# Four small expert rounds in plain fp32 with two column halves side by side, in the order L S L L S L S S

## The chip, the core and the metric

The kernel runs on one core of a Trainium2 chip. TensorE (PE), VectorE (DVE), ScalarE (ACT), GpSimd (POOL) and SyncE (SP) each run their own instruction stream and meet through semaphores; sixteen DMA engines move data between HBM and the core's memory. The metric is the device time of one execution, in microseconds, lower is better; the figure is the median of several runs.

## The reference

Two layers of a decoder trunk on 256 tokens of width 1024, all in float32. Layer 0 is attention (a dilated and a grouped-query part) and a dense SwiGLU of width 3584. Layer 1 is a gated linear recurrence and a mixture of eight SwiGLU experts, of which the router takes two for each token. What the change touches is the last part:

```python
def moe_swiglu(h, w_router, w_gate, w_up, w_down):
    ...
    logits = (t @ w_router).astype(jnp.float32)
    top_v, top_e = lax.top_k(logits, TOP_K)          # TOP_K = 2
    gates = jax.nn.softmax(top_v, axis=-1)
    ...
    def expert_block(args):                          # xb: rows of tokens, e: their expert
        xb, e = args
        return (jax.nn.silu(xb @ w_gate[e]) * (xb @ w_up[e])) @ w_down[e]
    ...
    y = yb.reshape(P, D)[dest] * g_sorted[:, None].astype(t.dtype)
    out = jax.ops.segment_sum(y, tok_sorted, num_segments=N)
```

An expert has three matrices of 1024 x 3584 floats, 44 MB together, and all eight are read: 352 MB. The result must agree with a float32 reference, so the kernel cannot round a factor to fewer bits and leave it there.

## The kernel before, in words

*The weight stream.* Every matrix is cut into units of 1 MB (128 partitions x 2048 floats). SyncE loads unit after unit into a ring of seven raw buffers (`raw`, `RAW = 7`, `load` at line 394; the transfer is line 408). A raw buffer may be overwritten when VectorE has split the unit that lay in it (`lo_done`).

*The split.* TensorE takes a float32 factor exactly in three fast passes if each factor is split into a high part, rounded to the fast format (`F32R`), and the rest. ScalarE copies each half of a unit to `w_hi` (lines 802 and 807), VectorE subtracts to get `w_lo` (lines 1229 and 1234). The split units lie in a ring of three (`SPL = 3`). `split_to(k)` on both engines makes them split ahead of TensorE by up to three units; PE's semaphore `unit_done` gives back a place.

*The products.* `triple` (lines 1870 to 1872) makes one product as high x high, high x low and low x high: three instructions with a stationary tile of 128 token rows and 512 streamed weight columns. A unit is four such products, 12 instructions. `pair` (lines 1876, 1877) does two instructions: where a block has at most 64 tokens, the high and the low part of the rows lie side by side in the 128 stationary columns, so that high and low of the weights are streamed once each, 8 instructions a unit, and the two halves of the output are added later.

*Rounds.* The router's counts put the experts in descending order of their tokens (`perm`; a place is a rank in this order). A round is one expert: 28 units of gate and up, then 14 units of down. Large rounds have 128 slots for tokens, small ones 64 (`HALF`). Before the change the places from 5 on are small (`SMALL_FROM = 5`), with up and down packed and gate as a triple. `phase` runs the gate and up products of the next round and the down products of the one before, interleaved from the fourth pair on: two gate or up units, one down unit. The order of rounds is written out in `BEFORE_LOOP`, `LOOP_PLACE` and `BEHIND_LOOP`: L S L, then the loop, which runs once when all counts fit their slots and nine times when one doesn't, then S L S L. Between the rounds GpSimd fetches the next round's token rows from HBM by an indirect DMA (`fetch`, line 669), PE transposes them (`row_transposes`), ScalarE copies the finished results to `ybuf` (`results`), and GpSimd stores them to `done` (`store_large`, line 679; `store_small`, two stores of which the second adds to the first, lines 690 and 692). At the end the other rounds' results are fetched back (line 739), weighted and added to X by VectorE (line 1812). The last round isn't stored: its results are brought to the token rows by a product with a one-hot matrix `ST`, in two fast parts (lines 2469 and 2473), and added (line 1825). Then follow the final norm and four stores of the output (line 471).

*Hidden rows.* The product silu(gate) x up of a round lies in `H` as rows; PE transposes it four blocks at a time (`expert_transposes`, line 2083), ScalarE and VectorE make `h_hi` and `h_lo` of it.

Plain float32 products exist before the change too: the weighting with `V` in attention (lines 2020 and 2022: 64 stationary columns, outputs in partitions 0-63 and 64-127 of one bank) and the sums with `ones` in the recurrence (line 2266). The profile records each plain float32 product as two instructions.

Of the kernel before, what the change touches and what calls it, by code (L numbers as in the profile page):

```python
# [75 lines left out]
FIRST_BLOCK = (0, 4, 5, 2, 15, 1, 3, 14)  # L76
# [4 lines left out]
SMALL_COL = BLOCKS  # L81
LAST_COL = 2 * BLOCKS
# [9 lines left out]
def behind_pair(pair):  # L92

    return 2 * (pair + 1) + max(0, pair - LAG)

# [9 lines left out]
class Tally:  # L105
# [3 lines left out]
    def __init__(self):  # L109
        self.count, self.per, self.var, self.rounds = {}, {}, None, 0  # L110
# [10 lines left out]
    def enter(self, var, per):  # L121
        self.var, self.per, self.start = var, per, dict(self.count)

    def leave(self, rounds):
# [3 lines left out]
        self.count, self.var = dict(self.start), rounds  # L128
# [16 lines left out]
def build(nc, x, positions, g_mix, g_ffn, g_final, w_in_attn, w_out_attn, attn_sinks, w_in_rec,  # L145
# [3 lines left out]
    with ctx:  # L149
# [36 lines left out]
        ST = sb("ST", [P, TOK], F32R)  # L186
# [17 lines left out]
        half_row = sb("half_row", [P, 2, 14], I32)  # L204
# [8 lines left out]
        behind_wait = sb("behind_wait", [P, 1], U32)  # L213
        token_now = sb("token_now", [P, 1], U32)
# [39 lines left out]
        y_hi = [t_lo[:, 4 * m:4 * m + 4, 0:CAP] for m in range(2)]  # L254
        y_lo = [t_lo[:, 4 * m:4 * m + 4, CAP:2 * CAP] for m in range(2)]
        beside = w_at(7680, 512).rearrange("p (s c n) -> p s c n", s=2, n=HALF)
        summed = w_at(8192, 512).rearrange("p (s c n) -> p s c n", s=2, n=HALF)
        h_pack = h_hi[:].rearrange("p s (c two n) -> p s c two n", two=2, n=HALF)
# [14 lines left out]
        back = [[w_at(5632, D), w_at(6656, D)], [w_at(10240, D), w_at(11264, D)]]  # L273
# [61 lines left out]
        y_half, yh_done, part_sq, bias_set = sem("y_half"), sem("yh_done"), sem("part_sq"), sem("bias_set")  # L335
# [5 lines left out]
        beside_done, sum_done, half_stored = sem("beside_done"), sem("sum_done"), sem("half_stored")  # L341
# [20 lines left out]
        for first in (2 * D, 3 * D):  # L362
            for nb in range(2):
# [3 lines left out]
        U0 = len(stream)  # L367
        assert FFN_UNITS % RAW == 0 and FFN_UNITS % SPL == 0
# [5 lines left out]
                     unit=FFN_UNITS)  # L374
# [12 lines left out]
        def _(sp):  # L387
            n = Tally()
# [4 lines left out]
            def load(src, k):  # L393

                seen = n.step("unit")
                if k >= RAW:
                    sp.wait_ge(lo_done, n.at("unit", RAW))
# [29 lines left out]
            def load_pair(e, pair, at):  # L427

                for h in range(2):
                    load(expert_unit(2 * pair + h, e), at + h)  # L430

            def load_phase(e_down, e_next):

                at = U0 + GU
                for pair in range(2 * FB):
                    load_pair(e_next, pair, at)
                    at += 2
                    if pair >= LAG:
                        load(expert_unit(GU + pair - LAG, e_down), at)
                        at += 1  # L440
                for j in range(2 * FB - LAG, DOWN):
                    load(expert_unit(GU + j, e_down), at)
                    at += 1

# [3 lines left out]
            e_down = 0  # L448
            for place, _ in BEFORE_LOOP[1:]:
                e_next = sp.value_load(perm[0:1, place:place + 1], min_val=0, max_val=NE - 1)  # L450
                load_phase(e_down, e_next)
                e_down = e_next
            before = sp.value_load(nrounds[0:1, 0:1], min_val=1, max_val=NE + 1)
            with sp.Fori(0, before) as i:
                n.enter(i, {"unit": FFN_UNITS})
                load_phase(sp.value_load(turn_of[0:1, bass.ds(i, 1)], min_val=0, max_val=NE - 1),
                           sp.value_load(turn_of[0:1, bass.ds(i + 1, 1)], min_val=0, max_val=NE - 1))
                n.leave(before)
            e_down = sp.value_load(turn_of[0:1, bass.ds(before, 1)], min_val=0, max_val=NE - 1)
            for place, _ in BEHIND_LOOP:  # L460
                e_next = sp.value_load(perm[0:1, place:place + 1], min_val=0, max_val=NE - 1)
                load_phase(e_down, e_next)
                e_down = e_next
            for j in range(DOWN):
                load(expert_unit(GU + j, e_down), U0 + GU + j)
# [10 lines left out]
        def _(pool):  # L476
# [36 lines left out]
            for m in range(2):  # L513
# [1985 lines left out]
```

## Time and profile before

| | |
|---|---|
| median of 3 runs | 1420.44 us (1420.31 to 1422.4) |
| the profiled execution, first to last instruction | 1416.6 us |
| mean granted TensorE clock in it | 0.997 |
| PE busy | 1384.1 us, 98% |
| VectorE busy | 1201.1 us, 85% |
| ScalarE busy | 997.2 us, 70% |
| DMA traffic | 452.48 MB, mean 319 GB/s |
| expert rounds, from the first gate product | about 513 to 1406 us |

A busy share is the union of an engine's instructions. PE's matmuls overlap in their pipeline, so the duration of one is longer than the distance to the next; what a matmul costs in a stream is the distance of starts. The page cuts the span in 40 slices of 35.4 us; the windows view gives busy time, clock, DMA share and GB/s for any stretch. A wait names the engine, the instruction that waited, and who released it.

### The profile page before, as it was taken

To read this page: it belongs to the slowest core of one execution; us is meant where nothing else is said; L and a number is where in the kernel's file an instruction comes from. 1 tells how busy PE (TensorE), PEld (TensorE's weight loads), DVE (VectorE), ACT (ScalarE), POOL (GpSimd) and SP (SyncE) were. 2 spreads that over 40 slices of the span, in tenths; PEclk is the share of its full clock that TensorE was granted. 3 is DMA by queue.
4 is the path that set the end of the run, shared out by engine and by line. 5 is a ranking of instruction groups with operands and counts; after the bars stand their busy time and mean duration, and the time that the engine had idled before them with its cause. 6 is when DMAs were issued, how large, how long until landed. Compare 5 with 4: busy or idle time off the path is not lost.

```text
span 1416.6 us, 19280 instructions
## 1 busy us (share of the span) xinstructions
PE 1384.1 (98%) x6746; PEld 1146.6 (81%) x6746; DVE 1201.1 (85%) x1455; ACT 997.2 (70%) x1247; POOL 165.1 (12%) x206
## 2 busy tenths in 40 slices
PE   8989999999999999999999999999999999999997
PEld 6858888888988887888888788888888878887876
DVE  7876554544887679999999999999999999999898
ACT  7666444444632577788888877788888888888885
POOL 1000200000244048300010000010020010010002
PEclk9999999999999999999999999999999999999999
DMA  9526785554543459999999999999999999999994
GB/s 333 203 66 203 289 335 183 201 175 154 179 149 110 158 142 393 403 409 409 410 408 410 409 407 406 387 375 410 406 412 412 407 406 413 409 411 414 399 415 155
DMA packets 134174, 452.48 MB, mean 319 GB/s; under 512 B 9514, under 2 KB 18818, under 8 KB 119744
## 3 DMA queue, kind: packets, MB, share of 16 engines
q1 hardware_dynamic: 126752, 433.09, 79.6%
q0 software_dynamic: 5456, 17.06, 3.3%
q10 hardware_dynamic: 1872, 1.12, 0.3%
q8 instruction: 54, 0.88, 0.2%
q14 instruction: 40, 0.33, 0.1%
HBM read 438.90 MB, written 14.17 MB: 320 GB/s over the span
## 4 chain that ended last, share of the span: by engine, by line
PE 76%; DVE 10%; DMA 3%; issue 3%; ACT 2%; DVEq 0%; ACTq 0%; SPq 0%
PE bank L1870 22%; PE bank L1872 21%; PE bank L1871 21%; DVE w_lo L1234 4%; DVE w_lo L1229 4%; DMA raw<-in_w_gate_moe_dram 3%; PE bank L1876 3%; PE bank L1877 3%; PE bank L2083 2%; PE bank L2258 1%; ACT w_hi L802 1%; DVE work L1493 1%; ACT w_hi L807 1%; PE bank L1891 1%; PE bank L2073 0%
## 5 line engine op out<-in xcount | busy, mean ns | idle before, releaser
L802 ACT ACTIVATE w_hi<-raw 128x1024 fp32r<-128x1024 f32 x411 | 435.4, 1059 | 352.5 <-PE bank L1872 325.7
L1229 DVE TENSOR_TENSOR w_lo<-raw,w_hi 128x1024 fp32r<-128x1024 f32 x411 | 506.1, 1231 | 145.0 <-ACT w_hi L802 143.7
L1234 DVE TENSOR_TENSOR w_lo<-raw,w_hi 128x1024 fp32r<-128x1024 f32 x411 | 506.7, 1233 | 0.1
L1870 PE MATMUL bank<-w_hi,t_hi 128*128 128x512 f32 (+1 forms) x1088 | 430.8, 396 | 2.4 <-DVE w_lo L1234 1.6
L807 ACT ACTIVATE w_hi<-raw 128x1024 fp32r<-128x1024 f32 x411 | 429.8, 1046 | 0.2 <-DMA raw<-in_w_in_attn_dram 0.2
L1871 PE MATMUL bank<-w_lo,t_hi 128*128 128x512 f32 (+1 forms) x1088 | 421.9, 388 | 0.0
L1872 PE MATMUL bank<-w_hi,t_hi 128*128 128x512 f32 x672 | 262.5, 391 | 0.0
L1870 PEld LDWEIGHTS bank<-w_hi,t_hi 128*128 128x128 f32 x1088 | 205.2, 189 | 44.7 <-issue 2.8
L1871 PEld LDWEIGHTS bank<-w_lo,t_hi 128*128 128x128 f32 x1088 | 204.9, 188 | 40.8 <-issue 1.0
L1872 PE MATMUL bank<-w_hi,t_lo 128*128 128x512 f32 (+1 forms) x472 | 182.3, 386 | 0.0
L1870 PE MATMUL bank<-w_hi,h_hi 128*128 128x512 f32 x408 | 162.7, 399 | 2.0 <-DVE w_lo L1229 1.6
L1872 PE MATMUL bank<-w_hi,h_lo 128*128 128x512 f32 x408 | 159.5, 391 | 0.0
L1871 PE MATMUL bank<-w_lo,h_hi 128*128 128x512 f32 x408 | 158.9, 390 | 0.0
L1872 PEld LDWEIGHTS bank<-w_hi,t_hi 128*128 128x128 f32 x672 | 126.2, 188 | 27.3
L1872 PEld LDWEIGHTS bank<-w_hi,t_lo 128*128 128x128 f32 x472 | 88.7, 188 | 18.3
L1870 PEld LDWEIGHTS bank<-w_hi,h_hi 128*128 128x128 f32 x408 | 76.7, 188 | 20.4 <-DVE w_lo L1229 3.7
L1872 PEld LDWEIGHTS bank<-w_hi,h_lo 128*128 128x128 f32 x408 | 76.6, 188 | 16.4
L1871 PEld LDWEIGHTS bank<-w_lo,h_hi 128*128 128x128 f32 x408 | 76.7, 188 | 14.8
L1876 PE MATMUL bank<-w_hi,h_hi 128*128 128x512 f32 x168 | 66.8, 398 | 4.8 <-ACT ST L1109 2.8
L1877 PE MATMUL bank<-w_lo,h_hi 128*128 128x512 f32 x168 | 65.9, 392 | 0.0
L676 POOL TENSOR_TENSOR slot_now<-slot_at,unit_of 128x1 uint32<-128x1 uint32 x4 | 5.0, 1260 | 412.5 <-ACT work L1093 412.5
L1876 PE MATMUL bank<-w_hi,t_hi 128*128 128x512 f32 x112 | 43.7, 390 | 0.0
(368 smaller groups left out, 1373.1 us busy)
## 6 DMA issues: line engine op xcount, KB each, us to landing
raw<-in_w_gate_moe_dram SPq DMA_DIRECT2D x112, 1024.0 KB, 9.3
raw<-in_w_up_moe_dram SPq DMA_DIRECT2D x112, 1024.0 KB, 9.5
raw<-in_w_down_moe_dram SPq DMA_DIRECT2D x112, 1024.0 KB, 9.7
raw<-in_w_in_rec_dram SPq DMA_DIRECT2D x16, 1024.0 KB, 5.5
raw<-in_w_gate_dense_dram SPq DMA_DIRECT2D x14, 1024.0 KB, 5.2
raw<-in_w_up_dense_dram SPq DMA_DIRECT2D x14, 1024.0 KB, 5.1
raw<-in_w_down_dense_dram SPq DMA_DIRECT2D x14, 1024.0 KB, 4.9
raw<-in_w_in_attn_dram SPq DMA_DIRECT2D x8, 1024.0 KB, 14.9
```

What stands on the lines that cost most here:

```text
L802: act.activation(w_hi[:, (u - 1) % SPL, half], raw[:, r, half], ACT.Copy).then_inc(hi_half, 1)
L807: act.activation(w_hi[:, (u - 1) % SPL, half], raw[:, r, half], ACT.Copy).then_inc(hi_done, 1)
L1229: dve.tensor_tensor(w_lo[:, s, half], raw[:, r, half], w_hi[:, s, half].bitcast(F32), ALU.subtract).then_inc(lo_half, 1)
L1234: dve.tensor_tensor(w_lo[:, s, half], raw[:, r, half], w_hi[:, s, half].bitcast(F32), ALU.subtract).then_inc(lo_done, 1)
L1493: dve.tensor_tensor(hb, hb, bank[up_bank][:], ALU.mult).then_inc(free[up_bank], 1)
L1870: pe.matmul(o, lh, rh, start=start, stop=False)
L1871: pe.matmul(o, lh, rl, start=False, stop=False)
L1872: return pe.matmul(o, ll, rh, start=False, stop=stop)
L1876: pe.matmul(o, packed, rh, start=start, stop=False)
L1877: return pe.matmul(o, packed, rl, start=False, stop=stop)
L1891: last = pe.transpose(bank[TB[j]][:, c * TOK + t * P:c * TOK + (t + 1) * P], rows_of[:, t, k * P:(k + 1) * P], ident[:])
L2083: last = pe.transpose(bank[b][:, c * P:(c + 1) * P], rows_h[:, c // 2, c % 2, :], ident[:])
```

## The change

The places from 4 on are small, four of eight; the order becomes L S L, the loop, S L S S. A small round no longer splits weights: PE multiplies straight from the raw buffers in plain float32, with 64 token columns as the stationary tile. Each token tile is used for two blocks of weight columns, whose products go to partitions 0-63 and 64-127 of one bank, one instruction behind the other. A list worked out when the program is built (`split_units`) says for each unit whether it is split or direct; ScalarE and VectorE skip the direct ones, SyncE waits for PE's count (`unit_done`) in place of VectorE's before it overwrites them. Rows, hidden rows and results of small rounds are kept in float32 (`t32`, `HS`, `h32`), without a high and a low part and without a sum of two halves. In a small round the results are 64 rows in two halves of the columns, and go out in two plain stores. The three units behind the loop that the loop's body has split ahead stay split, though nobody reads the parts. The last round is small, and its results are brought to the token rows in plain float32 from the two partition halves. Some small tables for the adding stores go.

```diff
-SMALL_FROM = 5
-BEFORE_LOOP = ((0, False), (5, True), (1, False))
+SMALL_FROM = 4
+BEFORE_LOOP = ((0, False), (4, True), (1, False))
 LOOP_PLACE = 2
-BEHIND_LOOP = ((6, True), (3, False), (7, True), (4, False))
-LAST_PLACE = 4
+BEHIND_LOOP = ((5, True), (3, False), (6, True), (7, True))
+LAST_PLACE = 7
...
+            def slot_given_back(k, loop):
...
+                if DIRECT[u]:
+                    sp.wait_ge(unit_done, past + (u + 1))
+                else:
+                    sp.wait_ge(lo_done, past + SPLITS[u])
...
+            def store_small(block):
+
+                for m in range(2):
+                    pool.dma_start(done_h[:, 2 * block, m * BLK:(m + 1) * BLK],
+                                   ybuf[m * HALF:(m + 1) * HALF, 0:BLK]).then_inc(y_stored, 16)
...
+                    if not n.in_loop and not SPLIT[u - 1]:
+                        continue
...
+            def gather_small():
+
+                wait_full(GATE + 1)
+                act.activation(t32, bank[GATE + 1][:], ACT.Copy).then_inc(free[GATE + 1], 1)
...
+            drained(GATE + 1, UP + 1)
+            dve.tensor_tensor(t32.rearrange("p (k n) -> p k n", k=KC), t_hi[:, :, 0:HALF].bitcast(F32),
+                              t_hi[:, :, CAP:CAP + HALF].bitcast(F32), ALU.add).then_inc(t32_done, 1)
...
+            dve.wait_ge(unit_done, n.past(here(DOWN)))
+            dve.tensor_copy(y32[:, BLK // 2:], bank[YLAST[1]][:, 0:BLK // 2]).then_inc(y_right, 1)
...
+            def raw_unit():
+
+
+                r = next_unit()
+                if SPLIT[n.count["at"] - 1]:
+                    pe.wait_ge(lo_done, n.at("split"))
+                pe.wait_ge(loaded[r], n.at(f"loaded{r}"))
+                return r
...
+            def small_down_unit(j):
+
+                if j % 4 == 0:
+                    drained(TR + j // 4 % 2)
+                r = raw_unit()
+                for k in range(2):
+                    for m in range(2):
+                        ws = slice(k * D + m * BLK, k * D + (m + 1) * BLK)
+                        last = pe.matmul(bank[YB][m * HALF:(m + 1) * HALF, :], small_columns(j, k), raw[:, r, ws],
+                                         start=j == 0 and k == 0, stop=j == DOWN - 1 and k == 1)
+                last.then_inc(unit_done, 1)
...
+            def small_pair(at):
...
+                for h in (2 * part, 2 * part + 1):
+                    r = raw_unit()
+                    for i in range(per):
+                        k = h * per + i
+                        for m in range(2):
+                            ws = slice((2 * i + m) * ncols, (2 * i + m + 1) * ncols)
+                            last = pe.matmul(bank[b][m * HALF:(m + 1) * HALF, 0:ncols], t32[:, k * HALF:(k + 1) * HALF],
+                                             raw[:, r, ws], start=k == 0, stop=k == KC - 1)
+                    last.then_inc(unit_done, 1)
...
+            for part, (ready, ns) in enumerate(((y_left, slice(0, BLK // 2)), (y_right, slice(BLK // 2, BLK)))):
+                pe.wait_ge(ready, 1)
                 for t in range(TT):
...
+                    for m in range(2):
+                        ms = slice(m * HALF, (m + 1) * HALF)
+                        last = pe.matmul(bank[LAST[t][m]][:, ns], ST[ms, t * P:(t + 1) * P], y32[ms, ns], start=True,
+                                         stop=True)
```

## Rows read from the trace of the kernel before

**Rows 1.** The page's second part, whole span: GB/s moved, 40 slices of 35.4 us.
```profile
GB/s 333 203 66 203 289 335 183 201 175 154 179 149 110 158 142 393 403 409 409 410 408 410 409 407 406 387 375 410 406 412 412 407 406 413 409 411 414 399 415 155
```
**Rows 2.** Windows, busy time of each engine by round (columns in the first line).
```profile
core 0: us, PE busy (x) PEld busy (x) DVE busy (x) ACT busy (x) POOL busy (x), PEclk, DMA share, GB/s
594.00:704.00 110.00, 109.37 (x500) 90.27 (x499) 107.27 (x103) 92.86 (x104) 0.00 (x0) 1.00 1.02 410
...
812.00:931.00 119.00, 119.00 (x543) 98.94 (x542) 109.71 (x103) 92.78 (x103) 3.93 (x5) 1.00 1.01 396
...
1146.00:1254.00 108.00, 107.40 (x486) 87.95 (x485) 106.50 (x102) 91.61 (x102) 6.26 (x5) 1.00 1.02 409
1254.00:1367.00 113.00, 108.21 (x484) 89.03 (x483) 106.08 (x107) 92.87 (x112) 4.20 (x4) 0.98 1.02 410
...
579.00:1390.00 811.00, 802.54 (x3636) 662.01 (x3635) 780.50 (x758) 673.98 (x770) 48.51 (x41) 1.00 1.02 406
```
**Rows 3.** ScalarE's timeline; a window; loads' time to landing, 1170-1300 us and dense part.
```profile
1200.41 1.06 ACT L802 ACTIVATE w_hi<-raw 128x1024 fp32r<-128x1024 f32 x1 [0.56 <-DMA raw<-in_w_gate_moe_dram]
...
1202.93 1.06 ACT L802 ACTIVATE w_hi<-raw 128x1024 fp32r<-128x1024 f32 x1 [0.51 <-DMA raw<-in_w_gate_moe_dram]
...
1170.00:1215.00 45.00, 45.00 (x205) 37.38 (x204) 44.12 (x42) 38.67 (x43) 0.00 (x0) 1.00 1.02 413
...
raw<-in_w_gate_moe_dram SPq DMA_DIRECT2D x18, 1024.0 KB, 13.6
...
raw<-in_w_up_dense_dram SPq DMA_DIRECT2D x14, 1024.0 KB, 5.1
```
**Rows 4.** Timeline of PE in the all-large round: start us, us, instruction.
```profile
847.50 0.39 PE L1870 MATMUL bank<-w_hi,t_hi 128*128 128x512 f32 x1
...
849.31 0.39 PE L1872 MATMUL bank<-w_hi,t_hi 128*128 128x512 f32 x1
```
**Rows 5.** The end: last load's issue and time to landing, then the engines' timelines.
```profile
1379.94 0.33 SPq L408 DMA_DIRECT2D raw<-in_w_down_moe_dram  x1
...
raw<-in_w_down_moe_dram SPq DMA_DIRECT2D x1, 1024.0 KB, 10.1
...
1405.19 0.39 PE L1872 MATMUL bank<-w_hi,h_lo 128*128 128x512 f32 x1
...
1400.83 5.24 DVE L1812 SCALAR_TENSOR_TENSOR X<-work,row_f,X 128x1024 f32<-128x1024 f32 x4
...
1407.39 2.73 DVE L1825 SCALAR_TENSOR_TENSOR X<-bank,gl,X 128x512 f32<-128x512 f32 x4
...
1412.13 1.81 SPq L471 DMA_DIRECT2D out_dram<-work  x4
```
**Rows 6.** The chain that ended last, at the two products of line 2266.
```profile
406.28 1.72 PE bank L2266 x4
```
**Rows 7.** Timelines of PE and its weight loads in attention; then line 2022's loads.
```profile
103.20 0.65 PE L2020 MATMUL bank<-work 128*64 128x256 f32 x4
103.68 0.39 PE L2022 MATMUL bank<-work 128*64 128x128 f32 x4
104.00 0.50 PE L1870 MATMUL bank<-w_hi,t_hi 128*128 128x512 f32 x1
...
103.47 0.36 PEld L2022 LDWEIGHTS bank<-work 128*64 128x64 f32 x4
...
L2022 PEld LDWEIGHTS bank<-work x32: 137/137/137, 62.6 to 103.7; 128*64 128x64 f32 x32
```
**Rows 8.** Line 739, the fetches of stored results: durations, first and last start, landing.
```profile
L739 POOL DMA_INDIRECT work<-done,row_from x4: 945/1424/1745, 1384.9 to 1390.2; - x4
...
DMA to landing us min/median/max: 5.8/6.0/6.4
```
**Rows 9.** A wait of PE in 1254 to 1367 us, and the window behind it.
```profile
PE bank L1876 <- ACT ST L1109: 2.8, 1, 2.8
...
1308.40:1311.80 3.40, 3.40 (x12) 2.74 (x11) 2.04 (x3) 2.00 (x2) 0.00 (x0) 0.53 1.03 418
```

More of the change, by code:

```diff
@@ L253, in build @@
         ybuf = w_at(4608, D)
[L254 to L258, printed above, removed]
+        t32 = w_at(12416, KC * HALF)
+        h32 = w_at(7680, 2 * BLK).rearrange("p (s n) -> p s n", s=2)
+        HS = w_at(5632, FF // 2)
+        y32 = t32
         key = w_at(10240, NE)
@@ L701, in _, with rows_taken @@
+            def rows_taken(r):
+                return U0 + GU + FFN_UNITS * (r - 2) + 2 * FB * 2 + 2 * FB - LAG
+            large = [sum(1 for small in SMALL_ROUND[:r] if not small) for r in range(LOOP_ROUND + 1)]
+            fetch(FIRST_BLOCK[BEFORE_LOOP[1][0]], 1)
             pool.wait_ge(unit_done, U0 + GU - 1)
             fetch(FIRST_BLOCK[BEFORE_LOOP[2][0]], 2)
-            results_ready(0)
-            store_large(FIRST_BLOCK[BEFORE_LOOP[0][0]], 1)
-            pool.wait_ge(unit_done, rounds_past)
@@ L767, in unit_at @@
             def unit_at(k):
[L768 to L769 removed]
+                return n.past(k + n.rounds * FFN_UNITS)
             def saw_product(*banks):
@@ L1093, in results @@
+            def gather_small():
+                wait_full(GATE + 1)
+                act.activation(t32, bank[GATE + 1][:], ACT.Copy).then_inc(free[GATE + 1], 1)
+            def results(small, stored_before):
+                act.wait_ge(y_stored, n.step("stored", stored_before))
+                banks = 1 if small else 2
+                saw_product(*(YB + m for m in range(banks)))
+                act.wait_ge(unit_done, n.past(here(FFN_UNITS)))
+                for m in range(banks):
                     act.activation(ybuf[:, m * BLK:(m + 1) * BLK], bank[YB + m][:], ACT.Copy).then_inc(free[YB + m], 1)
-                n.count["half"] = 2 * (start + AHEAD)
@@ L1745, in _, with here, up_rows @@
             start = U0 + GU
-            def up_rows(w, units):
+            def here(k):
+                return start + n.rounds * FFN_UNITS + k
+            def up_rows(w, units, small=False):
                 split_to(units + SPL)
+                if small:
+                    g, ns = (w + 1) % 2, slice(0, BLK if w < WIDE else BLK // 2)
+                    saw_product(GATE + g, UP + g)
+                    dve.wait_ge(unit_done, n.past(units))
+                    drained(GATE + g)
+                    hb = HS[:, w * BLK:w * BLK + ns.stop]
+                    dve.tensor_tensor(hb, hb, bank[UP + g][:, ns], ALU.mult).then_inc(free[UP + g], 1)
+                    return
@@ L1783, in _ @@
+                saw_product(YB)
+                if not small_down:
+                    saw_product(YB + 1)
+                if n.in_loop:
+                    n.count["half"] -= 2 * FFN_UNITS
             for w in range(WIDE):
```

631 lines of the change are left out of this document (341 added, 290 removed).

## The prediction, made before the kernel ran

> **What bounds the kernel now.** I read the page's slices first: from slice 17 on, which is the expert part, the DMA engines move 400 to 415 GB/s in nearly every slice, and nowhere in the kernel more [rows 1]. Then the windows round by round: PE is busy for 119 of 119 us in the round where both halves are large, and for 107 to 109 us in the others; VectorE for 104 to 110 us; the DMA share stands at 1.0 in all of them [rows 2]. Three resources lie within a few per cent of one another, so the question for each round is which is late last, and then what is late when that one is relieved.
>
> *DMA.* ScalarE's timeline at 1200 to 1203 us shows rounds in which it has nothing to do but wait for the next unit to land: its first halves start 2.52 us apart [rows 3]. A unit is 1.049 MB, and the same stretch moves 413 GB/s, which gives 2.54 us. There a load takes 13.6 us from issue to landing, against 5.1 us in the dense part, where the queue is empty [rows 3]: about five units stand in it, so nothing that an engine does makes it faster. A round of 42 units needs 42 x 2.54 = 106.7 us for weights alone, and with token rows and results some 109 to 110.
>
> *PE.* Eight starts of a split product lie between 847.50 and 849.31 us [rows 4]: 0.2265 us each. A large unit is 12 of them (three products x four), 2.72 us; a packed unit is 8, 1.81 us. All-large round: 42 x 2.72 = 114.2 us, and PE is busy for all of the 119 [rows 2], the other 4.8 us being transposes: there PE is the bound. Other rounds: 28 x 12 + 14 x 8 = 448 products, 101.5 us + 4.8 = 106: DMA and VectorE are just above it. So in six of the seven rounds PE's work is already about equal to what the stream delivers.
>
> *The end.* The last load is issued at 1379.94 and lands 10.1 us later, near 1390; PE ends its last unit at 1405.6 [rows 5]. These 15.6 us are backlog: 10 buffers (7 raw, 3 split) were full of work, and the last split goes at PE's pace. Behind it come 11.0 us of results, norm and store to 1416.6.
>
> **The change part by part.**
> (1) *Products of a small unit.* Instead of 12 (gate) or 8 (up, down) split products there are 4 plain fp32 ones with 64 stationary columns, of 512 columns each, in pairs that write different partition halves. Two plain fp32 products of 128 stationary columns and 512 streamed take 1.72 us in the chain (four instructions, each product being two) [rows 6], so 0.86 us each. Do the two of a pair run together? The attention part has this very shape: pairs of 128*64 products into partitions 0-63 and 64-127. Four instructions of 256 columns are over 0.65 us after they start; the next four of 128 columns end 0.22 us behind them (103.68 + 0.39 against 103.20 + 0.65) [rows 7]. In series the latter would need 4 x 128/512 x 0.43 = 0.43 us; 0.22 is half. So a pair costs what one costs, and a small unit 2 x 0.86 = 1.72 us. Nothing to split: VectorE and ScalarE lose two instructions each, 2.3 and 2.0 us a unit.
> The same rows bound the switch between full and half-wide products: the next full product starts 0.32 us after the 0.22 us group, so 0.1 us a switch. A mixed round has some 28 switches, 2.8 us, and stays below the stream as shown next. The Trainium skill (TensorEngine Tiling, Tiling Modes) says that changing the tiling mode drains TensorE; the trace agrees, with that 0.1 us.
>
> (2) *Rounds.* PE's need by round, as (gate/up, down): small/large 28 x 1.72 + 14 x 2.72 = 86 us; large/small 28 x 2.72 + 14 x 1.72 = 100 us; large/large 119; small/small 42 x 1.72 = 72 us. Order after: small/large, large/small, large/large, small/large, large/small, small/large, small/small, then 14 small down units. All but one are under the stream's 109 to 110, even with switches and 5 us of transposes. The relief of PE and VectorE there (20 us and more a round) is therefore worth almost nothing in those rounds: the next late thing, the stream, is 0 to 2 us behind. The all-large round stays at 119 on PE, but it now begins with little backlog, and 9 us more work than stream fits in the 10 buffers: the stream need not stop.
>
> (3) *The stream's own time.* In 579 to 1390 us before moves 406 GB/s x 811 us = 329.3 MB [rows 2]. After, the weights are the same; small results go out as two plain stores of 128 KB in place of two of 256 KB of which the second adds (some 0.8 MB less in three rounds); the four fetches of the results at the end (0.5 MB each), which now begin at 1384.9 [rows 8] and are mostly behind the last load, come ahead of it (1.5 MB more). 330.0 MB at 409.7 GB/s, the mean of undisturbed rounds (408 to 411 in [rows 2]), are 805.5 us: last landing near 1384.7. Bounds: at 413 [rows 3] 799 us, landing 1378; at 406 813 us, landing 1392. I take 1385, since 410 includes stores and fetches.
>
> (4) *Behind the last landing.* No split and no backlog: the stream is slower than PE, which waits for each unit. Last unit 1.7 + 0.1; copy of the right half 0.5; two pairs of 256 columns against the one-hot matrix 2 x 0.43 + 0.2, of which the first 0.65 stand before the first add; four adds 2.73 [rows 5]; and from the last add (1410.12) to the end 6.5 as before: 1.8 + 0.5 + 0.65 + 2.7 + 6.5 = 12.2 us. Before it was 26.6 from landing to end. The four adds of fetched results (5.24 us [rows 5], which now stand in the chain) are cheap only if the fetch is early: stores start when round 7 ends, 14 units = 35 us ahead of the last landing; before, two stores one behind the other and the fetches took from 1367 to 1396.2 (last issue 1390.2, landing 6.0 behind [rows 8]), 29 us. With adds 34: even unchanged this just fits, and the two stores now go together.
>
> (5) *New waits.* A raw buffer of a direct unit is returned when PE has read it, not when VectorE has split it (SyncE waits on PE's count). Behind the loop VectorE rebuilds the fp32 rows after three units split ahead, the last of them only when PE ended the round: some 2 + 1.3 + 0.7 = 4 us in which PE stands. Both are at nothing in the sum: queued loads (13.6 us deep) cover them. If the cover is gone, see below. GpSimd's stores and ScalarE's copies are fewer or equal. The one-hot wait of the last gate round costs PE 2.8 us now [rows 9]; it stays, under the stream.
>
> **Sum.** 1385 + 12.2 = 1397.2 us against 1416.6 of the profiled execution: -19.4 (5.0 from the stream, 14.4 from the end). The median of the runs is 3.8 us above that execution, so 1401.
>
> **Rivals.**
> *A, the ring stalls (slower loads, gain half lost).* A load needs 5.1 us from issue to landing in an empty queue [rows 3], so PE may be late by 7 x 2.54 - 5.1 = 12.7 us behind a landing before the stream stops. The all-large round begins with 3 to 5 us of lateness and adds 9, part (5) 4, a unit 1.7: 18 to 20, over by 5 to 7, and it may happen a second time behind the first round, which is all large too. Price 8 us: 1409. For it: the latenesses are known to 3 us only. Against: split units give their buffer back up to three units (8 us) ahead of PE, so most of this is covered.
> *B, weight loads are not hidden (slower).* The 64-column loads took 137 ns each [rows 7]. If the eight of a unit stood in the open, a unit costs 1.72 + 8 x 0.137 = 2.8 us, and the rounds turn PE-bound: 117, 115, 119, 117, 115, 117, 118, then 39: 857 us from 594, plus 10: 1461 + 4 = 1465. It decides from 2.5 us a unit. Against: the second group's loads start at 103.47, while the first group's products run until 103.85 [rows 7].
> The Trainium skill (TensorE: Matmul & The Clock Gate, Part 3, What overlaps and what doesn't) has loads overlap running products only when their row groups differ, and here both halves use the same rows. That is this rival. The trace speaks against it.
> *C, halves run one after the other with these sizes:* 3.44 us a unit, near 1570. Only if weight or data type matter in a way that 128*64 fp32 of the attention doesn't show.
> *D, nothing gained:* fetches end late and the four adds stand at the end again, and the stream runs at 406: 1392 + 12 + 5 + 3.8, and some stalls: 1417.
> *E, too many tokens:* a small round has 64 slots. The router's counts on these inputs, sorted, are 81, 70, 68, 67, 63, 56, 55, 52: the fifth, now small, has 63. With 65 the loop would run 8 more times, +950 us.
> *Clock:* the granted clock fell to its lower level, 1.2 GHz (0.53 of 2.4 in that window), for 3.4 us once, just after PE had stood for 2.8 us [rows 9]. After, PE stands 0.8 us a unit in the last 56 units. At half clock a unit takes 3.4 us, which makes PE busy again; it could cost 2 to 5 us at the very end. In the range.
>
> **How the numbers follow.** Forecast 1393 to 1408: 0.68. A: 0.14. D: 0.05. B: 0.07. C: 0.04. E and others: 0.02. The range takes in the stream's bounds (landing 1378 to 1392) and A with a late clock: 1393 to 1412, about 0.81. 0.2% is 2.8 us, about what can be told from no change. Faster by more (under 1417.6): 0.82; same 0.05; slower 0.13.
>
> **What would show it.** PE lines with 128*64 128x512, some 1100 instructions in pairs that start together, 0.43 us from pair to pair; small/small round near 107 us with PE busy 70%; ScalarE without work there; the stream at 409 to 412 GB/s in every slice to the end, with loads 13 us from issue to landing; last landing near 1385 and PE's last unit under 3 us behind it. Wrong if GB/s falls below 400 in rounds beside the all-large one (A), if PE is 100% busy in the small/small round (B, C), or if adds of fetched results stand in the chain at the end (D).

## The result, and the profile after

The changed kernel takes 1411.1 us in the median of 4 runs (1410.5 to 1412.1), the kernel before 1420.7 us on the same chip: a ratio of 0.9935, 95% interval 0.9922 to 0.9949. It is faster, as forecast, but by 9.6 us, half of what was forecast. The profiled execution has a span of 1409.7 us where 1397.2 had been worked out.

The page after, its first, second and part of its fifth section (for [rows 1]; a slice is now 35.2 us):
```profile
PE 1321.4 (94%) x6598; PEld 930.1 (66%) x6598; DVE 800.6 (57%) x1058; ACT 658.9 (47%) x865; POOL 145.0 (10%) x198
...
GB/s 337 202 65 205 284 341 182 194 175 167 178 152 94 156 146 361 393 407 410 408 413 413 407 413 412 401 291 415 406 411 413 406 414 413 406 414 413 408 418 251
...
L2570 PE MATMUL bank<-raw,work 128*64 128x512 f32 (+1 forms) x1024 | 208.9, 550 | 17.0 <-DMA raw<-in_w_up_moe_dram 12.6
```
VectorE lost 400 us of work and ScalarE 340, and the time moved by less than 10. That much was forecast: the stream sets the pace. The page also shows what was not: the 27th slice, which begins at 916 us, moves 291 GB/s, where those beside it move over 400.

The windows of the rounds after, for [rows 2]:
```profile
core 0: us, PE busy (x) PEld busy (x) DVE busy (x) ACT busy (x) POOL busy (x), PEclk, DMA share, GB/s
594.00:704.00 110.00, 104.19 (x492) 59.42 (x492) 48.15 (x48) 42.69 (x52) 4.56 (x6) 0.98 1.02 406
...
812.00:931.00 119.00, 114.78 (x518) 94.31 (x518) 108.41 (x103) 92.80 (x102) 7.42 (x10) 0.98 0.98 389
931.00:1038.00 107.00, 99.67 (x470) 55.09 (x467) 45.09 (x46) 39.38 (x46) 1.04 (x1) 0.99 0.99 393
...
1254.00:1367.00 113.00, 89.84 (x437) 30.11 (x436) 2.48 (x4) 7.02 (x14) 2.89 (x7) 1.00 1.02 413
...
920.00:945.00 25.00, 20.78 (x86) 9.50 (x87) 10.14 (x11) 9.74 (x13) 3.32 (x6) 0.86 0.67 241
```
The small/small round (1254 to 1367) is as drawn: PE busy for 80%, VectorE for 2%, the stream at its best. The two windows at the end of the all-large round and behind it are below 400, and the last window shows where: 241 GB/s over 25 us. At 413 those bytes would have taken 14.6 us, so the stream lost 10.4 there. The kernel before is slowed there too, but by less: in the same 25 us it moves
```profile
920.00:945.00 25.00, 25.00 (x115) 20.81 (x114) 22.49 (x23) 20.12 (x23) 4.00 (x6) 1.00 0.97 366
```
so the loss against it is (366 - 241) x 25 / 410 = 7.6 us.

The end after, for [rows 5]. The chain that ended last (start, us, what):
```profile
1377.87 19.11 DMA raw<-in_w_down_moe_dram
...
1397.02 1.95 PE bank L2270 x16
1398.96 1.50 PE bank L2641 x11
```
The timelines of VectorE and SyncE's queue:
```profile
1389.27 5.24 DVE L1901 SCALAR_TENSOR_TENSOR X<-work,row_f,X 128x1024 f32<-128x1024 f32 x4 [40.66 <-DMA work<-done,row_from]
...
1405.22 1.82 SPq L533 DMA_DIRECT2D out_dram<-work  x4
```
The last unit lands at 1377.87 + 19.11 = 1397.0 us, 7.0 later than before (1379.94 + 10.1 = 1390.0), and not 5 earlier. Behind it come 12.7 us, where before there were 26.6. So 13.9 us were gained behind the last landing, and 7.0 of them lost ahead of it: the profiled span is 6.9 us shorter. The medians differ by more than the spans, since the profiled execution of before lay 3.8 us below its median in span, and this one 1.4.

Where the 7.0 went, the timelines of PE, VectorE and SyncE's queue behind the loop show:
```profile
914.15 20.19 SPq L469 DMA_DIRECT2D raw<-in_w_up_moe_dram  x4
...
928.38 0.69 DVE L1891 TENSOR_TENSOR work<-t_hi 128x512 f32<-128x512 f32 x1
...
929.20 1.12 PE L2183 MATMUL bank<-ident,work 128*128 128x128 f32 x4 [4.22 <-DVE work L1891]
930.25 5.60 PE L2570 MATMUL bank<-raw,work 128*64 128x512 f32 x16
```
and the window behind the wait (columns as above):
```profile
930.30:933.70 3.40, 3.40 (x9) 0.95 (x10) 0.69 (x1) 0.60 (x1) 1.54 (x4) 0.50 0.39 119
```
PE stands for 4.22 us until VectorE has rebuilt the rows (line 1891), which sits behind the last split. When PE starts again the granted clock is at its lower level (0.50 of 2.4 GHz, 1.2 GHz), and its first two direct units take 5.60 us instead of 3.44. SyncE issues only four loads in 20.19 us, where a full stream wants eight, because the buffers that it waits for come back only when PE has read them. The stream runs dry: 119 GB/s in the last window. The waits of SyncE's queue from 912 to 936 us name PE:
```profile
SPq L469 <- PE bank L2570: 14.1, 2, 12.7
```
That is 14.1 us in two waits, one of 12.7.

### The profile page after: what moved, and what is told of

It is laid out like the page before. It is cut to its first block, busy times and chain, and to the rows that moved or that the text cites. A ratio compares the mean times of both kernels' runs of the same rounds, so it can differ in the third digit from the quotient of the medians.

```text
span 1409.7 us, 17733 instructions
## 1 busy us (share of the span) xinstructions
PE 1321.4 (94%) x6598; PEld 930.1 (66%) x6598; DVE 800.6 (57%) x1058; ACT 658.9 (47%) x865; POOL 145.0 (10%) x198
## 4 chain that ended last, share of the span: by engine, by line
PE 67%; DMA 21%; DVE 4%; ACT 1%; issue 1%; SPq 0%; DVEq 0%; ACTq 0%
PE bank L1975 18%; PE bank L1977 17%; PE bank L1976 17%; DMA raw<-in_w_down_moe_dram 15%; PE bank L2570 6%; PE bank L2254 3%; DMA raw<-in_w_up_moe_dram 3%; DMA raw<-in_w_gate_moe_dram 3%; DVE w_lo L1315 2%; PE bank L2393 1%; ACT w_hi L869 1%; DVE w_lo L1320 1%; PE bank L2183 1%; PE bank L1991 1%; PE bank L2173 0%
## 5 line engine op out<-in xcount | busy, mean ns | idle before, releaser
L1315 DVE TENSOR_TENSOR w_lo<-raw,w_hi 128x1024 fp32r<-128x1024 f32 x246 | 306.6, 1246 | 343.1 <-ACT w_hi L869 341.9
L869 ACT ACTIVATE w_hi<-raw 128x1024 fp32r<-128x1024 f32 x246 | 260.7, 1060 | 492.1 <-PE bank L1977 231.3
L1975 PE MATMUL bank<-w_hi,t_hi 128*128 128x512 f32 (+1 forms) x864 | 342.4, 396 | 4.4 <-DVE w_lo L1315 2.0
L1976 PE MATMUL bank<-w_lo,t_hi 128*128 128x512 f32 (+1 forms) x864 | 335.1, 388 | 0.0
L1320 DVE TENSOR_TENSOR w_lo<-raw,w_hi 128x1024 fp32r<-128x1024 f32 x246 | 307.2, 1249 | 0.6 <-ACT w_hi L875 0.6
L875 ACT ACTIVATE w_hi<-raw 128x1024 fp32r<-128x1024 f32 x246 | 256.9, 1044 | 0.8 <-DMA raw<-in_w_in_attn_dram 0.8
L2570 PE MATMUL bank<-raw,work 128*64 128x512 f32 (+1 forms) x1024 | 208.9, 550 | 17.0 <-DMA raw<-in_w_up_moe_dram 12.6
L1975 PEld LDWEIGHTS bank<-w_hi,t_hi 128*128 128x128 f32 x864 | 162.4, 188 | 51.1 <-issue 13.8
L1977 PE MATMUL bank<-w_hi,t_hi 128*128 128x512 f32 x448 | 174.7, 390 | 0.0
L1975 PE MATMUL bank<-w_hi,h_hi 128*128 128x512 f32 x352 | 144.7, 411 | 22.4 <-DVE w_lo L1315 22.2
L1976 PE MATMUL bank<-w_lo,h_hi 128*128 128x512 f32 x352 | 138.4, 393 | 0.0
L1977 PEld LDWEIGHTS bank<-w_hi,t_hi 128*128 128x128 f32 x448 | 84.1, 188 | 18.2
L2254 PE MATMUL bank<-raw,work 128*64 128x512 f32 x336 | 80.0, 603 | 7.5 <-DMA raw<-in_w_down_moe_dram 7.5
L1976 PEld LDWEIGHTS bank<-w_lo,h_hi 128*128 128x128 f32 x352 | 66.8, 190 | 12.2
```

Source lines behind the costliest of these rows:

```text
L869: act.activation(w_hi[:, (n.count["split"] - 1) % SPL, half], raw[:, r, half], ACT.Copy).then_inc(hi_half, 1)
L875: act.activation(w_hi[:, (n.count["split"] - 1) % SPL, half], raw[:, r, half], ACT.Copy).then_inc(hi_done, 1)
L1315: dve.tensor_tensor(w_lo[:, s, half], raw[:, r, half], w_hi[:, s, half].bitcast(F32), ALU.subtract).then_inc(lo_half, 1)
L1320: dve.tensor_tensor(w_lo[:, s, half], raw[:, r, half], w_hi[:, s, half].bitcast(F32), ALU.subtract).then_inc(lo_done, 1)
L1975: pe.matmul(o, lh, rh, start=start, stop=False)
L1976: pe.matmul(o, lh, rl, start=False, stop=False)
```

## Experiments

Two theories at the start. *Mine:* the stream is the bound; it lost some 10 us behind the loop because PE's lateness there reached SyncE through the ring of raw buffers, and some 5 us to the fetches of results that now go among the last loads. *The rival:* the change itself, or PE in general, slows the stream (other traffic, the plain products), and the small rounds' PE work sets the end. All times are medians beside runs of the kernel before on the same chip, which took 1420.0 to 1421.5 us; beside the changed kernel it took 1420.7, so a difference of under 1 us to 1411.1 says nothing. Landings, windows and chains are those of one profiled execution each.

**1. Rebuild the rows early.** The sum of the two halves is put into the loop's body, right behind the gather, so that PE finds it ready; the first lines below stand there, the others are the old place.
```diff
+                    if n.in_loop:
+                        drained(GATE + 1, UP + 1)
+                        dve.tensor_tensor(t32.rearrange("p (k n) -> p k n", k=KC), t_hi[:, :, 0:HALF].bitcast(F32),
+                                          t_hi[:, :, CAP:CAP + HALF].bitcast(F32), ALU.add).then_inc(t32_done, 1)
...
-            drained(GATE + 1, UP + 1)
-            dve.tensor_tensor(t32.rearrange("p (k n) -> p k n", k=KC), t_hi[:, :, 0:HALF].bitcast(F32),
-                              t_hi[:, :, CAP:CAP + HALF].bitcast(F32), ALU.add).then_inc(t32_done, 1)
...
-            pe.wait_ge(t32_done, 1)
+            pe.wait_ge(t32_done, before)
```


> The changed kernel, with the float32 rows for the round behind the loop rebuilt inside the loop's body, as soon as they have arrived, and not behind the three units split ahead. Theory (the stream of weights is the bound, and the wait of 4.2 us at the start of that round, with the lower clock behind it, stopped it for 9.7 us): PE's wait goes, the load that was issued at 933.8 us is issued near 927.7, the stream's gap there falls from 12.3 to about 6 us, and the time by 6 us, to 1405. Rival (the gap is made up later, or PE's lateness at the end of the all-large round alone stops the stream): no change, 1411.


Measured: 1407.1 us (1406.2 to 1407.3), ratio 0.9899 [0.9883, 0.9916], 4.0 us better than the change. A window and the chain of this kernel:
```profile
920.00:945.00 25.00, 25.00 (x117) 12.83 (x117) 12.99 (x13) 10.31 (x13) 2.98 (x6) 1.00 0.88 330
```
```profile
1373.74 19.11 DMA raw<-in_w_down_moe_dram
```
PE no longer stands (25.00 of 25 us busy), its clock stays at 1.00, and the window moves 330 GB/s instead of 241. The last landing is 1392.9, 4.1 earlier, and the end follows by as much. It is 2 us short of the expectation: 330 is not 410, and what is left belongs to PE's lateness from the loop itself, as experiments 2 and 9 show. This kernel computes the whole reference and is the fastest version that does.

**2. Less PE work in the all-large round.** Its product of the weights' high part with the rows' low part is left out.
```diff
-                pe.matmul(o, lh, rl, start=False, stop=False)
+                if not n.in_loop:
+                    pe.matmul(o, lh, rl, start=False, stop=False)
```


> The changed kernel with two of the three split products in the all-large round (it leaves out the high x low products there, so 38 us of PE's work, and the output lacks them). Theory (stream bound; that round costs only because PE comes out of it some 15 us late): the stream doesn't stop at all, minus 9.7 us, 1401. Rival (the 119 us of PE in that round stand in the total): minus 38 us, 1373.


Measured: 1406.1 us (1404.9 to 1407.8), ratio 0.9898 [0.9882, 0.9915]; last landing 1371.02 + 19.10 = 1390.1. Some 38 us of PE work (42 units x 4 x 0.2265) were taken away and 5 us came back, 5 fewer than expected. PE's timeline, and the window:
```profile
923.00 1.12 PE L2184 MATMUL bank<-ident,work 128*128 128x128 f32 x4 [6.29 <-DVE work L1891]
```
```profile
920.00:945.00 25.00, 22.00 (x96) 9.40 (x98) 7.21 (x8) 5.31 (x9) 3.93 (x6) 0.86 0.88 341
```
PE comes to the end of the loop early and then waits for the rebuilt rows all the same: the wait grew to 6.29 us. So the stop has two causes in a row, PE's lateness and the wait for VectorE, and each alone keeps a little under half of it: at 410 GB/s the 25 us lost 10.3 us in the change, 4.9 in experiment 1 and 4.2 here.

**3. No fetches.** The four fetches of stored results and the four adds of them are left out.
```diff
-            for t in range(TT):
-                for r in range(2):
-                    pool.indirect_dma_start(out=back[t][r], out_offset=None, in_=done,
-                                            in_offset=bass.IndirectOffsetOnAxis(ap=row_from[:, t, r:r + 1], axis=0)
-                                            ).then_inc(y_back, 16)
...
-            dve.wait_ge(y_back, 16 * 2 * TT)
-            for r in range(2):
-                for t in range(TT):
-                    link(dve.scalar_tensor_tensor(X[:, t, :], back[t][r], row_f[:, 3, t, r:r + 1], X[:, t, :],
-                                                  ALU.mult, ALU.add))
```


> The changed kernel without the four fetches of the stored results and without their adds (the other rounds' results are missing in the output). Theory (the fetches now run ahead of the last loads and take their share of the DMA engines): units 400 to 406 land 2.5 us apart and not 3.7, minus 5.3 us, 1406. Rival (they are hidden, as the sum had them for the most part): minus 1 or less, 1410 to 1411.


Measured: 1406.3 us, ratio 0.9893 [0.9876, 0.9909]. The chain ends with a last load of 15.11 us instead of 19.11:
```profile
1377.96 15.11 DMA raw<-in_w_down_moe_dram
```
That is a last landing of 1393.1, 3.9 earlier, and 4.8 us less time. This execution began the expert rounds late, though: the first gate product starts at 515.14, where the change has 513.40, so from there on 5.6 us were gained. The fetched 2.1 MB, 5.1 us at 410 GB/s, cost about what they weigh. The adds themselves cost nothing: in the change they start at 1389.27 and are over before the last unit lands.

**4 and 5. Is PE's relief worth anything by itself?** In the kernel before, the small rounds' second product is left out (first diff); in the kernel after, half of the products of all direct units but the last 14 (second diff, in `small_pair` and in `small_down_unit`).
```diff
-                pe.matmul(o, packed, rh, start=start, stop=False)
-                return pe.matmul(o, packed, rl, start=False, stop=stop)
+                return pe.matmul(o, packed, rh, start=start, stop=stop)
```

```diff
-                    for i in range(per):
+                    for i in range(0, per, 2):
...
-                for k in range(2):
+                for k in range(1):
```


> The kernel before with one product in place of two in its packed units (the low part of the weights is left out there, so 76 us of PE's work in the small rounds). Theory (the stream bounds the small rounds of before already): minus 2 to 6 us, 1415 to 1419, and that from less backlog at the end. Rival (PE bounds before in its small rounds too): minus 30 to 76 us, 1345 to 1390.


Measured: 1418.8 us (10 runs), ratio 0.9987 [0.9977, 0.9996]. 76 us of PE work less, 2 us gained: PE was not the bound of the kernel before in these rounds. VectorE, busy for 106 to 107 us of each too [rows 2], was not relieved here. That it was not the bound either follows from the DMA share of 1.02, and from the changed kernel: with VectorE's work gone from the small/small round the stream moves 413 GB/s, where it moved 410.

> The changed kernel with one pair of products in place of two in the direct units of all rounds but the last 14 units (half the products of small rounds are left out, 130 us of PE's work). Theory (the stream and its one stop bound the time): the first small unit behind the loop is over 0.9 us sooner, so minus 1 to 2 us, 1409 to 1411. Rival (PE's small units stand in the total): minus 50 us and more, under 1360.


Measured: 1409.7 us (1408.1 to 1411.5), ratio 0.9926 [0.9909, 0.9942], not to be told from the change. The rival theory, in which PE's work in the small rounds sets the end, falls with these two.

**6. More PE work in the direct units.** Three pairs instead of two in each.
```diff
-                    for i in range(per):
+                    for n_i, i in enumerate([*range(per // 2), *range(per)]):
...
-                for k in range(2):
+                for n_k, k in enumerate((0, 0, 1)):
```


> The changed kernel with three pairs in place of two in the same units (one product in three is done twice, so 2.58 us a unit). Theory (a small unit is free up to about 2.4 us, since a mixed round also has 3 to 5 us of transposes and 3 us of switches): PE becomes the bound in every round, 117 us in five mixed ones, 119 and 111 in the others, 1460 us. Rival (only the stream and its stops count until 2.54 us a unit are passed by much): under 1425.


Measured: 1475.1 us (one run), span 1473.4.
```profile
594.00:704.00 110.00, 110.00 (x549) 54.83 (x549) 39.48 (x40) 32.72 (x39) 0.00 (x0) 1.00 0.97 368
```
PE is busy for all of the window and the stream has fallen to 368 GB/s. So a unit of 2.58 us does decide the time; rival B's limit of 2.5 was, if anything, too high. Most of the 15 us over the estimate come from a fuller sum: the units of the rounds are 819 us, transposes (4.8 us in six rounds) and switches (2.8 in five) 43, and 594 + 819 + 43 + 12 = 1468 for the span. Some 3 more stand at the end, where the last unit is there at 1457.4 and 16.0 us follow instead of 12.7: here the adds of the fetched results do stand in the chain (rival D's end), since what they fetch lands only then.
```profile
1457.57 5.25 DVE L1901 SCALAR_TENSOR_TENSOR X<-work,row_f,X 128x1024 f32<-128x1024 f32 x4 [41.07 <-DMA work<-done,row_from]
```

**7. Are the two of a pair really side by side?** Both write partitions 0-63, so that they can't be.
The same edit is made in line 2254.
```diff
-                            last = pe.matmul(bank[b][m * HALF:(m + 1) * HALF, 0:ncols], t32[:, k * HALF:(k + 1) * HALF],
-                                             raw[:, r, ws], start=k == 0, stop=k == KC - 1)
+                            last = pe.matmul(bank[b][0:HALF, 0:ncols], t32[:, k * HALF:(k + 1) * HALF],
+                                             raw[:, r, ws], start=k == 0 and m == 0, stop=k == KC - 1 and m == 1)
```

> The changed kernel with both products of each pair written to partitions 0 to 63, so that they use the same half of the array (the output lacks the other half's blocks; the last 14 units are as they were). Theory (the two of a pair ran together, 0.86 us, and now run one after the other, 1.72): 3.44 us a unit, PE-bound rounds of 134, 129, 119, 134, 129, 134 and 144 us, 1570 us in all. Rival (they did not run together, and the rows of the attention part had another reason): no change, 1411.


Measured: 1605.3 us (one run), span 1603.5, 194 us more than the change. Below, PE in this kernel, then PE in the changed one (start, us, instructions):
```profile
1504.93 7.03 PE L2570 MATMUL bank<-raw,work 128*64 128x512 f32 x16
```
```profile
936.46 10.52 PE L2570 MATMUL bank<-raw,work 128*64 128x512 f32 x48
946.91 0.50 PE L1975 MATMUL bank<-w_hi,h_hi 128*128 128x512 f32 x1
```
A unit is eight recorded instructions. In one half, two units take 6.9 us; in two halves, six units and the switch to split products take 946.91 - 936.46 = 10.45, which is 1.74 each. The 35 us over the estimate are mostly the same 43 us of transposes and switches. A fuller sum (an estimate from the same rows) has 915 us for the units of the rounds, 36 for the last 14, which were left as they are and come at the stream's pace, and 594 + 915 + 36 + 43 + 12 = 1600 for the span.

**8. A ring of six raw buffers** instead of seven.
```diff
-RAW = 7
+RAW = 6
```


> The changed kernel with six raw buffers in place of seven. Theory (the stream stops when PE is later behind a landing than the ring allows, 7 x 2.54 less 5 to 6 us from issue to landing): the allowance falls by 2.5 us, so the stop behind the loop grows from 9.7 to 12.2 us, and PE's waits of 4 to 6 us in the mixed rounds stay covered: plus 2.5 to 4 us, 1414 to 1415. Rival (the ring has nothing to do with it, the stop is the wait alone): no change, 1411.


Measured: 1416.1 us (1413.9 to 1418.6), ratio 0.9963 [0.9951, 0.9976], 5 us slower than the change.
```profile
920.00:945.00 25.00, 20.78 (x84) 11.67 (x84) 13.44 (x14) 10.22 (x13) 3.31 (x6) 0.86 0.65 222
```
```profile
1388.58 15.56 DMA raw<-in_w_down_moe_dram
```
PE's time behind the loop (20.78 us busy) and its clock are those of the change, and the last landing is 7.1 later (1404.1). But most of that does not come from the stop. PE's first gate product of the experts, in the change and then here:
```profile
513.40 0.47 PE L1975 MATMUL bank<-w_hi,t_hi 128*128 128x512 f32 x1 [0.73 <-issue]
...
515.37 0.47 PE L1975 MATMUL bank<-w_hi,t_hi 128*128 128x512 f32 x1 [0.73 <-issue]
```
The experts begin 2.0 us late, and with one unit less in the ring when they begin, the stream is another 2.5 us behind (an estimate, one unit). The two windows round the stop:
```profile
812.00:931.00 119.00, 117.37 (x532) 97.16 (x530) 110.29 (x103) 94.85 (x105) 5.45 (x5) 1.00 1.01 396
931.00:1038.00 107.00, 94.97 (x443) 50.62 (x444) 40.11 (x41) 35.01 (x44) 3.31 (x6) 0.97 0.95 375
```
The change moves 389 and 393 GB/s in them, 1.1 MB more, which is 2.7 us at 410. So one buffer less does make the stop longer, by about the 2.5 us of one unit that the theory wanted: the depth of the ring has a part in turning PE's lateness into time. The 5 us of the median cannot be read as the price of that, since a ring of six costs time ahead of the experts as well.

**9 to 11. Do the parts add up?** Experiments 1 and 2 together, 1 and 3 together, and all three.

> The fp32 rows are rebuilt in the all-large round's loop body, as in rows_early, and that round makes two of its three split products, as in loop_two (its output is not the reference's: the product of the weights' high part with the rows' low part is left out there). My theory: the stream stopped behind that round by PE's lateness plus PE's stand for the rebuilt rows. Each alone left some 5 us of the 9.7 us stop, since the other remained. With both gone no gap between two landings is over 3.5 us there, the last landing comes 3 us ahead of loop_two's 1389.9, near 1387, and the time is 1402 to 1404. Rival: the 5 us that stay in each come from something else (token rows and stores that share the stream); then it lands at 1390 as loop_two did, 1405 to 1407.


Measured: 1405.2 us (1404.2 to 1405.6), ratio 0.9893 [0.9873, 0.9914]; last landing 1370.23 + 19.40 = 1389.6.
```profile
920.00:945.00 25.00, 20.43 (x88) 8.94 (x86) 7.28 (x9) 6.32 (x10) 3.88 (x6) 0.93 1.02 404
1360.00:1390.00 30.00, 20.84 (x170) 12.13 (x172) 5.14 (x4) 2.47 (x4) 4.08 (x5) 1.00 0.81 336
```
The stop is gone (404 GB/s, DMA share 1.02), so that part of the theory stands. But the last landing is only 0.5 us ahead of experiment 2's and the time is the rival's number. Of the 3.8 us that the window gained over experiment 2 ((404 - 341) x 25 / 410), about 1 went again in later windows: from 945 to 1146 us they move 408 instead of 410 and 411. Why, the runs do not show. Some 2 more went at the very end. First experiment 2, then this run:
```profile
1380.00:1385.00 5.00, 3.89 (x32) 2.12 (x32) 2.72 (x3) 0.00 (x0) 0.00 (x0) 1.00 0.96 401
1385.00:1390.00 5.00, 3.90 (x32) 2.32 (x32) 2.42 (x2) 0.00 (x0) 0.00 (x0) 1.00 0.32 133
...
1380.00:1385.00 5.00, 3.51 (x32) 1.83 (x29) 2.39 (x2) 0.00 (x0) 0.00 (x0) 1.00 0.65 269
1385.00:1390.00 5.00, 3.97 (x36) 2.38 (x34) 2.75 (x3) 0.00 (x0) 0.00 (x0) 1.00 0.18 75
```
The DMA share falls well before the last unit lands, so some, and then most, of the sixteen engines have nothing left while the others still carry the last loads. At the 418 GB/s of the 10 us before, the bytes behind 1380 us would have been in by 1384.1, and the last landing is 5.5 us behind that; in experiment 2 it is 3.7 behind. The bytes came sooner, the last of them did not. Why the engines end so unevenly is not shown.

> The fp32 rows are rebuilt in the all-large round's loop body, as in rows_early, and the four fetches of the results and their four adds are left out, as in no_fetch (its output is not the reference's). My theory: the stop of the stream and the fetches in the stream are two separate losses of 4 to 5 us each, so they add up: 1411 minus 4.0 minus 4.8, 1402 to 1403, last landing near 1388. Rival: what one frees the other takes; then it stays at 1406.


Measured: 1402.8 us (1401.1 to 1403.6), ratio 0.9874 [0.9853, 0.9895]; last landing 1389.1. The two losses are separate: 4.0 and 4.8 alone, 8.3 together.

> All three together: rows rebuilt early, two of three products in the all-large round, no fetches and no adds of results (its output is not the reference's). My theory: this is the stream that I had forecast, with nothing that stops it and without the fetches' 2.1 MB: last landing near 1382 (early_two's 1387 minus 5), time 1397 to 1399. Rival: the stream itself is slower in this kernel than in the kernel before (the extra stores, other addresses); then it lands at 1387 or later, 1402 or more.


Measured: 1399.9 us (1398.7 to 1400.8), ratio 0.9854 [0.9833, 0.9875]; last landing 1371.12 + 15.12 = 1386.2. The time lies between the two expectations, nearer to mine; the landing is nearer to the rival's. The landing is 4 us behind my 1382, but this execution began the experts 2.3 us later than the change did:
```profile
515.74 0.47 PE L1966 MATMUL bank<-w_hi,t_hi 128*128 128x512 f32 x1 [0.73 <-issue]
```
So from there on the stream with nothing in its way is some 2 us slower than I had put it.

## Why the prediction was right and wrong, point by point

*Direction and bound: right.* That the stream and not PE bounds both kernels in the small rounds is shown by experiments 4 and 5 (PE work taken away, 2 us or less gained) and, for the changed one, by 6 (added, and the stream falls below 400 GB/s); VectorE is out by the DMA share and by the small/small round, as said under experiment 4.

*Step (1), the unit: right.* 1.72 us forecast, 1.74 with its share of a switch measured. Rivals B and C are out: with loads in the open a unit would have been 2.8 us, and one after the other it is 3.44, as experiment 7 shows (1605 us). The Trainium skill (TensorE: Matmul & The Clock Gate, Part 3: Packing small matmuls) has weight loads overlap running products only when their row groups differ. Here both products of a pair use all rows, and the trace does not agree. The line's loads (count, then min/median/max in ns):
```profile
L2570 PEld LDWEIGHTS bank<-raw,work x1024: 132/137/230, 595.3 to 1347.5; 128*64 128x64 f32 x171
```
Eight of them would be 1.1 us, and the unit is as long as its products alone.

*Step (2), the rounds: right for six, wrong for the all-large one.* It said "the stream need not stop". It stopped.

*Step (4), behind the last landing: right.* 12.2 us forecast, 12.7 measured, against 26.6 before. The adds of fetched results were over in time, so rival D did not come.

*Step (5) is the one that failed.* It put both new waits at nothing, since "queued loads (13.6 us deep) cover them". The 4 us of standing were sized right (4.22 measured). But the same text, under rival A, had the room as 12.7 us and the lateness as 18 to 20, and set that aside because split units give their buffers back ahead of PE. They do, until the direct units come: the buffers that SyncE needed behind the loop were to be given back by PE alone, and PE was late: the first unit behind the loop had landed at 912.4 by its load's semaphore, and PE began to read it at 930.25, 18 us later. That is the lateness that rival A had, and over its 12.7 us of room. Rival A was what happened. Its price of 8 us was near: experiments 1 and 2 together take 7.4 us off the last landing (1397.0 to 1389.6). Its chance of 0.14 was far too low for a sum that already came out over the limit. What it adds, that this may happen a second time behind the first round, came too, but small. From 594 to 620 us, before and after:
```profile
594.00:620.00 26.00, 25.44 (x118) 20.91 (x117) 24.40 (x24) 21.45 (x24) 0.00 (x0) 1.00 1.03 412
594.00:620.00 26.00, 26.00 (x121) 12.31 (x121) 7.48 (x8) 5.69 (x7) 0.29 (x1) 1.00 0.98 393
```
That is 1.2 us of the stream, and SyncE's waits of 583 to 606 us name PE here too:
```profile
SPq L469 <- PE bank L2570: 12.6, 5, 6.7
```
The clock made it worse: the forecast had the fall to 1.2 GHz only for the end, and it came behind this wait.

*Step (3), the stream's own time: 5 us too short.* 1385 forecast for the last landing; with both causes of the stop gone it is 1389.6. The 1.5 MB of fetches ahead of the last landing were in the sum, and experiment 3 confirms their price (5.6 us with its late start taken off, for 2.1 MB). What was off is the rate: 409.7 GB/s was taken from undisturbed rounds and used up to the last landing. Two stretches are not like the rounds that it was taken from. Behind the first round the stream slows where the first direct units come (385 GB/s in 594 to 620 us in experiment 9, 412 before: 1.7 us). And at the end it does not run full to the last landing, which comes 5.5 us behind the time that its bytes would need at 418. These two are more than the 4.6 that are missing; the small/small round, at 413, gives some back. How the rest divides is open.

*The sum.* Landing +12.0 (7.4 from step (5), 4.6 from step (3)), tail +0.5: 12.5 us, which is 1409.7 against 1397.2. Against the median it is 10.1, since the offset from profiled span to median was taken as 3.8 and is 1.4 here.

## What to carry to other kernels

When a change moves the point at which a buffer is given back from a fast engine to a late one, compare that engine's lateness at the worst place with what the ring covers, and if the sum is over the limit, believe it: one stop of the stream took 7.4 us back out of the 13.9 that were gained at the end, while 400 us of work saved on VectorE bought next to nothing in the rounds themselves. A small step that an engine needs at the start of a new phase belongs ahead of the queue in which it would stand last; moving one add of 0.69 us brought 4.0 us. When two profiled executions are compared, look first where the stage that matters begins in each: here that differed by up to 2.3 us, half of what some experiments were to show. And take the offset between a profiled execution and the median from several runs, not from one.

## What the runs showed of the hardware that I had not expected

- Plain float32 products with 64 stationary columns run in pairs at the price of one, from the same 128 rows, with their weight loads hidden: 1.74 us for four products of 512 columns, 3.44 us when both write the same half.
- PE's clock fell to its lower level behind a stand of 4.22 us (0.50 in the 3.4 us that followed) and behind none when the wait was removed. With half of the direct products left out (experiment 5) it stayed there for much of the small/small round:
```profile
1254.00:1367.00 113.00, 78.05 (x267) 21.13 (x268) 2.48 (x4) 6.41 (x12) 4.37 (x7) 0.71 1.02 413
```
```profile
1299.09 1.97 PE L2254 MATMUL bank<-raw,work 128*64 128x512 f32 x4 [0.60 <-DMA raw<-in_w_down_moe_dram]
```
Half the instructions (four) there take as long (1.97 us) as all eight do at full clock (1.95 in the chain of the change), so PE looks almost as busy as in the change (78 us against 90), with half of the work. A busy share without its clock would have hidden this.
- While PE is not the bound, the stream's pace in that round does not depend on PE's work or clock: 413 GB/s in the change (PE busy 90 us at full clock) and in experiment 5.
- The last landing can stand well behind the last full stretch of the stream: in experiment 9 the DMA share is 0.65 from 1380 to 1385 us and 0.18 from there to 1390, and the last load lands at 1389.6.
